# Rows of the first expert tile selected on TensorE, with shorter routing arithmetic

## The chip, the cores and the metric

The kernel runs on one core of one Trainium2 chip. The metric is the time of one execution on the device in microseconds (us). TensorE does the matrix products, VectorE and ScalarE the elementwise work, GpSimd starts the indexed transfers, SyncE starts the large loads. Times inside the program are taken from one profiled execution and count from the start of its span.

## The reference, cut to what matters

A block of 512 tokens of width 1024: a modulated norm, a mixing layer, a residual sum, a second modulated norm that gives `hf`, and a mixture of 16 experts of which each token takes two. Only the last part is touched.

```
def grouped_moe(h, router_w, router_bias, w_gate, w_up, w_down):
    logits = t @ router_w                              # 512 x 16
    probs = softmax(logits); sel = (probs + bias) in 4 groups of 4
    group_score = sum of the 2 best of each group; g_idx = argmax
    e_idx = the 2 best experts of that group
    wts = probs of these two, divided by their sum
    a = silu(t @ w_gate[e]) * (t @ w_up[e]) * combine[:, e]
    y = sum over e of a @ w_down[e]
```

## The kernel before

All arithmetic is float32. A wide product is made of three passes (`three`, L1363 to L1365): each operand is split into a rounded part "hi" (type float32r, made on ScalarE) and a remainder "lo" (made on VectorE, L771), and hi*hi, hi*lo and lo*hi are summed in PSUM. Weights arrive in `raw` (six slots of 128x2048) and their two parts stand in `wsplit` (six slots as well).

The stage in question lies between 424 and 481 us. TensorE transposes the normed rows `hf` (L1548) and makes the router logits (L1537). VectorE then does the routing: softmax, `rank` of the four experts of each group (L1103 to L1113; six instructions, with two comparisons and two multiplications by a table `order` so that ties fall the right way), the sum of the two best, `rank` of the four groups, and the mask of chosen experts `r_m` (L1130). From the mask TensorE counts each token's place in its expert's list (L1562, L1564, with full float32 operands), and VectorE writes the place to `pos1` (L1151).

Tokens are handled in tiles of 128 rows of one expert. Tile 0 is expert 0's first 128 rows, tile 1 expert 1's; the rest of the table (which expert and which rows each of the up to 24 tiles has, in `expert_of`, `base`, `weights_of`) is worked out on VectorE (L1183 to L1229) and released with `tiles_ready`. For every tile the steps are:

- VectorE makes a selection matrix `sel` (`select`, L1160: four instructions of 128x128, one for each 128 tokens);
- TensorE multiplies it with `info` (`index`, L1573), which gives the token number, weight and destination of each row; VectorE copies them out (`indices`, L1168 to L1170);
- GpSimd gathers the rows of `hf` from a copy in HBM into `hg` (`gather`, L461);
- TensorE turns the rows (`turn`, L1583), ScalarE writes the hi part of `hgT` (L683), VectorE the lo part (`rows_lo`, L1175);
- TensorE makes gate and up (`gate_up`: four chunks of 12 products with 512 columns), the hidden part is formed (L1238), turned (L1617) and multiplied by the down weights.

The order on each engine is written by hand. On TensorE it is `index(0,0)`, `index(1,1)`, `turn(0)`, `gate_up(0)`, then `index(2)`, `turn(1)`, `turn_hidden(0)`, then `gate_up(1)` and the loop. On VectorE, the selection of tile 0 comes first, then the table in pieces, with the lo parts of the two up chunks of tile 0 (`lo_n(M0 + 2)`, `lo_n(M0 + 3)`) among them; after `tiles_ready` come `select(2)`, three lo parts, `hidden(0)`, `indices(2)`, a fourth lo part and `rows_lo(1)`, on which `gate_up(1)` waits (`hg_lo`).

Semaphores count finished steps: `hi_ready`, `lo_ready` (split chunks), `chunk_used` (products done with a chunk), `sel_ready`, `idx_mm`, `idx_ready`, `gathered`, `hg_t`, `hg_hi`, `hg_lo`. `step` and `done` on VectorE chain dependent small instructions.

## Time and profile before

| | us |
|---|---|
| median of three runs | 804.03 |
| lowest and highest | 803.33, 804.06 |
| the profiled execution, whole | 805.07 |
| its span | 803.3 |
| TensorE matmul busy in the span | 735.6 (92%) |
| VectorE busy | 589.2 (73%) |
| ScalarE busy | 389.6 (49%) |
| GpSimd busy | 192.8 (24%) |

The profiled execution took 1.04 us more than the median. The span is what the trace covers. Busy shares are means over stages with different limits, so the stage around a change has to be read from the trace: the chain of waits says which engine released which, the timeline gives the instructions of one engine in order, and a table of stretches gives busy time and the TensorE clock that was granted (1.00 is 2.4 GHz, 0.50 is 1.2 GHz).

### The profile page before, as it was taken

To read this page: it belongs to the slowest core of one execution; us is meant where nothing else is said; L and a number is where in the kernel's file an instruction comes from. 1 tells how busy PE (TensorE), PEld (TensorE's weight loads), DVE (VectorE), ACT (ScalarE), POOL (GpSimd) and SP (SyncE) were. 2 spreads that over 40 slices of the span, in tenths; PEclk is the share of its full clock that TensorE was granted. 3 is DMA by queue.
4 is the path that set the end of the run, shared out by engine and by line. 5 is a ranking of instruction groups with operands and counts; after the bars stand their busy time and mean duration, and the time that the engine had idled before them with its cause. 6 is when DMAs were issued, how large, how long until landed. Compare 5 with 4: busy or idle time off the path is not lost. (4 is left out here: it accounts for less than half of the span.)

```text
span 803.3 us, 10622 instructions
## 1 busy us (share of the span) xinstructions
PE 735.6 (92%) x3359; PEld 606.1 (75%) x3360; DVE 589.2 (73%) x789; ACT 389.6 (49%) x352; POOL 192.8 (24%) x79
## 2 busy tenths in 40 slices
PE   2589999999999999999998389999999999999990
PEld 2468888866888888886788278888888888888880
DVE  3762344765485766668464788999999999999955
ACT  6442523343323241415234266777777777777723
POOL 1000001401000000000062101445555555444532
PEclk9689999999999999999997589999999999999996
DMA  8796330431365564726464428599999999999685
GB/s 323 271 371 218 104 131 15 143 104 53 107 217 179 171 216 138 280 87 259 160 227 142 163 79 310 203 354 407 370 358 375 358 360 380 371 373 381 249 170 165
DMA packets 105651, 187.66 MB, mean 234 GB/s; under 512 B 6991, under 2 KB 50063, under 8 KB 105628
## 3 DMA queue, kind: packets, MB, share of 16 engines
q1 hardware_dynamic: 98076, 173.58, 59.6%
q0 software_dynamic: 5936, 12.14, 5.5%
q10 hardware_dynamic: 1616, 1.65, 0.6%
q8 instruction: 13, 0.21, 0.1%
q14 instruction: 10, 0.08, 0.0%
HBM read 180.47 MB, written 16.25 MB: 245 GB/s over the span
## 5 line engine op out<-in xcount | busy, mean ns | idle before, releaser
L771 DVE TENSOR_TENSOR wsplit<-raw,wsplit 128x2048 fp32r<-128x2048 f32 x132 | 298.9, 2284 | 81.0 <-ACT wsplit L521 53.5
L700 ACT ACTIVATE wsplit<-raw 128x2048 fp32r<-128x2048 f32 x96 | 184.0, 1920 | 73.5 <-PE ps L1365 73.5
L469 POOL DMA_INDIRECT expert_rows<-work,dest_now x15 | 108.2, 7210 | 113.5 <-DVE work L1256 113.5
L1363 PE MATMUL ps<-wsplit,hgT 128*128 128x512 f32 x280 | 112.7, 403 | 5.0 <-DVE hgT L1175 5.0
L1365 PE MATMUL ps<-wsplit,hgT 128*128 128x512 f32 x280 | 110.9, 396 | 0.0
L1364 PE MATMUL ps<-wsplit,hgT 128*128 128x512 f32 x280 | 110.6, 395 | 0.0
L1363 PE MATMUL ps<-hT,wsplit 128*128 128x512 f32 x256 | 101.0, 395 | 1.0 <-DVE mx L929 1.0
L1365 PE MATMUL ps<-hT,wsplit 128*128 128x512 f32 x256 | 99.6, 389 | 0.0
L1364 PE MATMUL ps<-hT,wsplit 128*128 128x512 f32 x256 | 99.6, 389 | 0.0
L828 DVE SCALAR_TENSOR_TENSOR raw<-raw,c_silu 128x256 f32 (+1 forms) x128 | 62.0, 484 | 12.9 <-DMA raw<-in_w_ada 8.9
L1363 PEld LDWEIGHTS ps<-wsplit,hgT 128*128 128x128 f32 x280 | 53.7, 192 | 16.5 <-DVE hgT L1175 5.7
L1365 PEld LDWEIGHTS ps<-wsplit,hgT 128*128 128x128 f32 x280 | 53.5, 191 | 11.8
L1364 PEld LDWEIGHTS ps<-wsplit,hgT 128*128 128x128 f32 x280 | 53.8, 192 | 10.9
L1363 PE MATMUL ps<-wsplit,hT 128*128 128x512 f32 x128 | 52.8, 412 | 8.3 <-DVE hT L877 6.8
L477 POOL TENSOR_TENSOR wsplit<-raw,wsplit 128x2048 fp32r<-128x2048 f32 x2 | 9.2, 4610 | 200.6 <-ACT wsplit L521 200.5
L1363 PEld LDWEIGHTS ps<-hT,wsplit 128*128 128x128 f32 x256 | 48.1, 188 | 11.7 <-issue 1.9
L640 ACT ACTIVATE wsplit<-raw 128x2048 fp32r<-128x2048 f32 x16 | 30.7, 1918 | 53.4 <-PE ps L1365 34.8
L1364 PEld LDWEIGHTS ps<-hT,wsplit 128*128 128x128 f32 x256 | 48.1, 188 | 10.4 <-issue 0.7
L521 ACT ACTIVATE wsplit<-raw 128x2048 fp32r<-128x2048 f32 x20 | 38.2, 1915 | 36.5 <-PE ps L1365 14.0
L1365 PEld LDWEIGHTS ps<-hT,wsplit 128*128 128x128 f32 x256 | 48.0, 188 | 10.1
L1364 PE MATMUL ps<-wsplit,hT 128*128 128x512 f32 x128 | 51.8, 405 | 0.0
L1365 PE MATMUL ps<-wsplit,hT 128*128 128x512 f32 x128 | 51.8, 404 | 0.0
(257 smaller groups left out, 1190.5 us busy)
## 6 DMA issues: line engine op xcount, KB each, us to landing
raw<-in_w_exp_gate SPq DMA_DIRECT2D x32, 1024.0 KB
raw<-in_w_exp_up SPq DMA_DIRECT2D x32, 1024.0 KB
raw<-in_w_exp_down SPq DMA_DIRECT2D x32, 1024.0 KB
raw<-in_w_ada SPq DMA_DIRECT2D x24, 1024.0 KB
raw<-in_w_in SPq DMA_DIRECT2D x20, 1024.0 KB
expert_rows<-tmp SPq DMA_DIRECT2D x4, 1024.0 KB, 12.3
raw<-in_w_branch_a SPq DMA_DIRECT2D x4, 1024.0 KB
raw<-in_w_branch_b SPq DMA_DIRECT2D x4, 1024.0 KB
```

Source lines behind the costliest of these rows:

```text
L469: g.indirect_dma_start(out=y_dram, out_offset=bass.IndirectOffsetOnAxis(ap=dest_now[:, 0:1], axis=0), in_=y, in_offset=None, bounds_check= ...
L477: g.tensor_tensor(wsplit[:, c + 2, 1, :], raw[:, c + 2, :], wsplit[:, c + 2, 0, :].bitcast(F32), ALU.subtract).then_inc(lo_ready, 1)
L521: A_(wsplit[:, n, 0, :], raw[:, slot, :], ACT.Copy).then_inc(hi_ready, 1)
L640: A_(wsplit[:, (j + 1) % 2, 0, :], raw[:, (j + 1) % 4, :], ACT.Copy).then_inc(hi_ready, 1)
L700: A_(wsplit[:, c, 0, :], raw[:, c, :], ACT.Copy).then_inc(hi_ready, 1)
L771: V.tensor_tensor(wsplit[:, n, 1, :], raw[:, slot, :], wsplit[:, n, 0, :].bitcast(F32), ALU.subtract).then_inc(lo_ready, 1)
L828: ins = V.scalar_tensor_tensor(out=acc, in0=raw[:, slot, k * CC:(k + 1) * CC], scalar=c_silu[:, k:k + 1], in1=acc, op0=ALU.mult, op1=ALU.add)
L1363: nc.tensor.matmul(out, w_hi, m_hi_, start=first, stop=False)
L1364: nc.tensor.matmul(out, w_hi, m_lo_, start=False, stop=False)
L1365: return nc.tensor.matmul(out, w_lo, m_hi_, start=False, stop=last)
```

## The change

- Tile 0's rows are no longer gathered. After the second norm ScalarE writes the hi part of each 128 rows of `hf` to `wsplit` slots 1 and 0 and VectorE the lo part (`hf_part`; 4 copies and 4 subtractions of 128x1024). TensorE multiplies them with the selection matrix `sel_first` (`first_rows`: 2 halves x 2 parts x 4 blocks x 4 token groups = 64 products with 128 columns), which gives the turned rows at once. Hi and lo parts are copied out by ScalarE and VectorE, 512 columns at a time.
- `index(0,0)` and `index(1,1)` move behind the first chunk of `gate_up(0)`, which is written out so that its chunks wait for halves of the rows.
- The ranking is a subtraction, one comparison with a table `beats` (0 or the least normal number) and a sum. A threshold and a multiplication become one instruction in two places.
- The place products take float32r operands (`before_r`, `ones_r`, `r_mask`).
- On VectorE the selection of tile 0 comes before the weights' arithmetic, and the whole table comes behind the rows of tile 0; `lo_n(M0 + 3)` moves ahead of the table's last part.
- SyncE waits also for the lo parts of `hf` before it loads over `hf`. Semaphore counts of `gathered` are one less.

```
@@ sync
             sp.wait_ge(hf_t, 2 * NT)
+            sp.wait_ge(hs_lo, NT)
             for c in range(2):
                 load(c + 4, w_up[0, :, 4 * c:4 * c + 4, :], 4)
@@ gpsimd
-            for j in range(4):
+            for j in range(1, 4):
                 gather(j)
@@ scalar
+            def rows_split(t):
+                act.wait_ge(hf_ready, t + 1)
+                act.wait_ge(chunk_used, O0 + 2 if t < 2 else M0 - 1)
+                A_(hf_part(t, 0), hf[:, t, :], ACT.Copy).then_inc(hs_hi, 1)
...
-            rows_hi(0)
+            for half in range(2):
+                act.wait_ge(row0_mm, 2 * half + 1)
+                A_(hgT[:, 0, 4 * half:4 * half + 4, :].rearrange("p k m -> p (k m)"), ps[:, 2 + half, :],
+                   ACT.Copy).then_inc(hg_hi if half else row0_hi, 1)
+            act.wait_ge(hg_t, 1)
@@ vector
+            for t in range(NT):
+                dve.wait_ge(hs_hi, t + 1)
+                V.tensor_tensor(hf_part(t, 1), hf[:, t, :], hf_part(t, 0).bitcast(F32),
+                                ALU.subtract).then_inc(hs_lo, 1)
...
-                step(V.tensor_tensor(r_ge[:, 0:n], other, mine, ALU.is_ge))
-                step(V.tensor_tensor(r_gt[:, 0:n], other, mine, ALU.is_gt))
+                step(V.tensor_tensor(r_ge[:, 0:n], other, mine, ALU.subtract))
...
+                step(V.tensor_tensor(r_ge[:, 0:n], r_ge[:, 0:n], beats[:, :, :].unsqueeze(1).broadcast_to(pair),
+                                     ALU.is_ge))
...
+            def first_rows_lo(half):
+                dve.wait_ge(hg_t if half else row0_mm, 1 if half else 2)
+                V.tensor_copy(hgT[:, 1, 4 * half:4 * half + 4, :].rearrange("p k m -> p (k m)"),
+                              ps[:, 5 + half, :]).then_inc(hg_lo if half else row0_lo, 1)
@@ tensor
-            nc.tensor.matmul(ps[:, 2, 0:(NT + 1) * E], before[:, :], r_m_all, start=True, stop=False)
+            nc.tensor.matmul(ps[:, 2, 0:(NT + 1) * E], before_r[:, :], r_mask[:, :], start=True, stop=False)
...
-            index(0, 0)
-            index(1, 1)
-            turn(0)
-            gate_up(0, M0, 2)
+            def first_rows(half):
+                for part in range(2):
+                    for k in range(4 * half, 4 * half + 4):
+                        for t in range(NT):
+                            mm = nc.tensor.matmul(ps[:, (2, 5)[part] + half, (k % 4) * P:(k % 4 + 1) * P],
+                                                  hf_part(t, part)[:, k * P:(k + 1) * P], sel_first[:, t, :],
+                                                  start=(t == 0), stop=(t == NT - 1))
+                    mm.then_inc(hg_t if half and part else row0_mm, 1)
+
+            pe.wait_ge(sel_ready, 1)
+            pe.wait_ge(hs_lo, NT)
+            first_rows(0)
+            first_rows(1)
+            for c in range(4):
+                half = c % 2
+                pe.wait_ge(hg_hi if half else row0_hi, 1)
+                pe.wait_ge(hg_lo if half else row0_lo, 1)
+                pe.wait_ge(lo_ready, M0 + c + 1)
+                for k in range(4):
+                    kk = 4 * half + k
+                    mm = three(ps[:, c // 2, :], hgT[:, 0, kk, :], hgT[:, 1, kk, :],
+                               wblock(2 + c, 0, k, 512), wblock(2 + c, 1, k, 512), kk == 0, kk == ND - 1)
+                mm.then_inc(chunk_used, 1)
+                if c == 0:
+                    index(0, 0)
+                    index(1, 1)
```

How this moves instructions is seen at two places. The first is TensorE from the place products to the start of tile 0's gate product. In these rows `ps<-info,sel` are the index products and `ps<-ident,work` the turning of gathered rows. Before:

```order
L1562 MATMUL ps<-work,before 128x80
L1564 MATMUL ps<-work,ones 128x64
L1564 MATMUL ps<-work,ones 128x48
L1564 MATMUL ps<-work,ones 128x32
L1564 MATMUL ps<-work,ones 128x16
L1573 MATMUL ps<-info,sel 128x4 x8
L1583 MATMUL ps<-ident,work 128x128 x8
L1363 MATMUL ps<-wsplit,hgT 128x512
```

On TensorE after, from the same place (`ps<-sel_first,wsplit` are the 64 selecting products):

```order
L1606 MATMUL ps<-r_mask,before_r 128x80
L1608 MATMUL ps<-r_mask,ones_r 128x64
L1608 MATMUL ps<-r_mask,ones_r 128x48
L1608 MATMUL ps<-r_mask,ones_r 128x32
L1608 MATMUL ps<-r_mask,ones_r 128x16
L1676 MATMUL ps<-sel_first,wsplit 128x128 x64
L1407 MATMUL ps<-wsplit,hgT 128x512
```

The eight index products have left this place; they stand twelve gate products later, on TensorE after the first chunk:

```order
L1409 MATMUL ps<-wsplit,hgT 128x512
L1622 MATMUL ps<-info,sel_first 128x4 x4
L1622 MATMUL ps<-info,sel 128x4 x4
L1407 MATMUL ps<-wsplit,hgT 128x512
```

The second place is VectorE behind the selection of tile 0, where L771 (before) and L798 (after) are the lo parts of weight chunks. Before, the selection of tile 1 and the first part of the table stand ahead of tile 0's rows:

```order
L1160 TENSOR_SCALAR sel<-iota,base,pos 128x128 x4
L1189 TENSOR_TENSOR work<-work 128x16
L1190 TENSOR_SCALAR work<-work 128x16
L1192 TENSOR_TENSOR work<-work 128x16
L1194 TENSOR_SCALAR work<-work 128x1
L1196 MEMSET work 128x1
L1198 SCALAR_TENSOR_TENSOR work<-ones,work 128x16
L771 TENSOR_TENSOR wsplit<-raw,wsplit 128x2048
L1203 TENSOR_TENSOR work<-iota,work 128x384
L1206 TENSOR_REDUCE work<-work 128x24
L1208 TENSOR_TENSOR work<-work 128x384
```

On VectorE after, the rows of tile 0 (L1223, twice) come first, and the table starts behind them:

```order
L1198 TENSOR_SCALAR sel<-iota,base,pos 128x128 x4
L1223 CAST hgT<-ps 128x512
L798 TENSOR_TENSOR wsplit<-raw,wsplit 128x2048
L1223 CAST hgT<-ps 128x512
L1230 TENSOR_SCALAR work<-work 128x16
L1231 TENSOR_SCALAR work<-work 128x16
L1232 TENSOR_SCALAR work<-work 128x16
L1234 TENSOR_TENSOR work<-work 128x16
L1235 TENSOR_SCALAR work<-work 128x16
L1237 TENSOR_TENSOR work<-work 128x16
L1239 TENSOR_SCALAR work<-work 128x1
L1241 MEMSET work 128x1
```

What moved: the whole table now stands behind the second row copy, which waits for the last of the 64 products; before it stood mostly beside the gather.

## Rows read from the trace of the kernel before

**Rows 1.** Chain of waits, 452 to 481 us: start, us, engine and line.

```profile
452.58 5.03 DMA work<-hf_rows,tok_idx
457.65 1.98 PE ps L1583 x8
...
461.99 0.80 PE ps L1363
...
467.90 0.30 PE ps L1364
...
475.72 0.24 PE ps L1365
...
480.32 0.50 PE ps L1363
```

**Rows 2.** Stretches: length, busy PE, PEld, DVE, ACT, POOL, PEclk, DMA, GB/s.

```profile
480.00:485.00 5.00, 4.68 (x14) 3.69 (x15) 5.00 (x4) 2.52 (x4) 0.00 (x0) 0.66 0.27 46
...
600.00:760.00 160.00, 160.00 (x778) 133.92 (x777) 159.45 (x158) 117.70 (x79) 85.87 (x18) 1.00 0.97 362
```

**Rows 3.** Timeline of VectorE, routing: start, us, operation, idle before it.

```profile
441.26 0.42 DVE L1103 TENSOR_TENSOR work<-work 128x256 f32<-128x256 f32 x1
...
443.77 0.19 DVE L1121 TENSOR_SCALAR work<-work 128x64 f32<-128x64 f32 x1
...
444.51 0.22 DVE L1103 TENSOR_TENSOR work<-work 128x64 f32<-128x64 f32 x1
...
446.02 0.22 DVE L1130 TENSOR_TENSOR work<-work 128x64 f32<-128x64 f32 x1
...
448.65 0.22 DVE L1151 SCALAR_TENSOR_TENSOR pos<-ps,work 128x64 f32<-128x64 f32 x1 [0.30 <-PE ps L1564]
...
448.99 1.11 DVE L1160 TENSOR_SCALAR sel<-iota,base,pos 128x128 fp32r<-128x128 f32 x4
```

**Rows 4.** Timeline of TensorE: place products and logits.

```profile
430.63 3.60 PE L1537 MATMUL ps<-router,work 128*128 128x16 f32 x16 [0.25 <-ACT work L245]
...
446.80 1.81 PE L1564 MATMUL ps<-work,ones 128*128 128x64 f32 x8
```

**Rows 5.** Timelines of VectorE, ScalarE and SyncE, 431 to 440 us.

```profile
439.48 0.23 DVE L1083 TENSOR_REDUCE work<-ps 128x4 f32<-128x64 f32 x1 [7.92 <-PE ps L1537]
...
435.19 0.60 ACT L245 ACTIVATE work<-ps 128x512 f32<-128x512 f32 x1 [4.13 <-PE ps L1548]
...
436.26 0.94 SPq L278 DMA_DIRECT2D raw<-in_w_exp_up  x2
```

**Rows 6.** All instructions of L1452: duration, first and last start, form.

```profile
L1452 PE MATMUL ps<-tmp,raw x64: 270/275/275, 130.7 to 137.7; 128*128 128x128 f32 x64
```

**Rows 7.** Stretches of 1 us at the kernel's start (columns as in rows 2).

```profile
14.00:15.00 1.00, 0.90 (x5) 0.93 (x6) 0.95 (x2) 1.00 (x2) 0.00 (x0) 1.00 1.06 412
...
18.00:19.00 1.00, 1.00 (x12) 1.00 (x11) 0.96 (x3) 0.00 (x0) 0.00 (x0) 1.00 1.06 412
```

**Rows 8.** Timeline of VectorE, table and tile 1.

```profile
452.49 0.17 DVE L1189 TENSOR_TENSOR work<-work 128x16 f32<-128x16 f32 x1
...
453.57 2.29 DVE L771 TENSOR_TENSOR wsplit<-raw,wsplit 128x2048 fp32r<-128x2048 f32 x1
455.78 0.55 DVE L1203 TENSOR_TENSOR work<-iota,work 128x384 f32<-128x384 f32 x1
...
461.85 0.54 DVE L1212 TENSOR_REDUCE work<-work 128x24 f32<-128x384 f32 x1
...
463.71 2.29 DVE L771 TENSOR_TENSOR wsplit<-raw,wsplit 128x2048 fp32r<-128x2048 f32 x1
465.92 1.11 DVE L1160 TENSOR_SCALAR sel<-iota,base,pos 128x128 fp32r<-128x128 f32 x4
...
476.04 0.69 DVE L1238 TENSOR_TENSOR work<-ps,work 128x512 f32<-128x512 f32 x1 [0.77 <-PE ps L1365]
...
476.85 2.28 DVE L771 TENSOR_TENSOR wsplit<-raw,wsplit 128x2048 fp32r<-128x2048 f32 x1
```

More of the change, by code:

```diff
@@ L45 @@
 SKIP = 2048
+LEAST = 1.1754943508222875e-38
 FIN_X = (4, 5, 6, 8)
@@ L93, in tokens_moe_kernel @@
         mx = sb("mx", [P, NT * D])
+        with nc.sbuf_tensor("sel_first", [P, NT, P], F32R) as sel_first:
+            pass
         tmp = sb("tmp", [P, 2 * D])
         iota1 = sb("iota1", [P, P])
+        before_r = sb("before_r", [P, P], F32R)
+        ones_r = sb("ones_r", [P, P], F32R)
+        r_mask = sb("r_mask", [P, (NT + 1) * E], F32R)
         router = sb("router", [P, ND, E])
@@ L108, in tokens_moe_kernel @@
         bias_row = sb("bias_row", [P, E])
-        order = sb("order", [P, 2, EG, EG])
+        beats = sb("beats", [P, EG, EG])
         pos1 = sb("pos1", [P, NT, E])
@@ L180, in tokens_moe_kernel @@
                   "pos_mm", "tiles_ready"))
+        hs_hi, hs_lo, row0_mm, row0_hi, row0_lo, info_ready = map(
+            sem, ("hs_hi", "hs_lo", "row0_mm", "row0_hi", "row0_lo", "info_ready"))
         sel_ready, idx_mm, idx_ready, gathered, hg_t, hg_hi, hg_lo = map(
@@ L215, in tokens_moe_kernel @@
         r_gs, r_gr = small(NT * EG), small(NT * EG)
-        r_ge, r_gt = (small(NT * E * EG).rearrange("p (g a b) -> p g a b", a=EG, b=EG) for _ in range(2))
+        r_ge = small(NT * E * EG).rearrange("p (g a b) -> p g a b", a=EG, b=EG)
         r_cnt, r_x, r_x2, r_x3, r_cum = (small(E) for _ in range(5))
@@ L237, in mix_lo, with hf_part @@
                                        op1=ALU.subtract).then_inc(yb_lo, 1)
+        def hf_part(t, part):
+            return wsplit[:, 1 - t // 2, part, (t % 2) * D:(t % 2 + 1) * D]
         def turned(act, activation, t):
@@ L424, in _ @@
             g.memset(eps_col[:, :], EPS)
-            g.memset(order[:, :, :, :], 1.0)
+            g.memset(beats[:, :, :], 1.0)
             g.iota(iota_i[:, :], pattern=[[1, P]], base=1, channel_multiplier=0)
@@ L459, in gather @@
                 wait_reg(pool, idx_ready, j + 1)
-                wait_reg(pool, hg_t, j, 0)
+                if not isinstance(j, int) or j > 1:
+                    wait_reg(pool, hg_t, j)
                 g.indirect_dma_start(out=hg, out_offset=None, in_=hf_dram,
@@ L672, in _ @@
                    scale=1.0 / D).then_inc(rooted, 1)
-            for t in range(2, NT):
-                turned(act, A_, t)
+                if t:
+                    rows_split(t - 1)
+            turned(act, A_, 2)
+            rows_split(NT - 1)
+            turned(act, A_, 3)
             act.wait_ge(sub_ready, 1)
@@ L1077, in _ @@
             step(V.memset(r_m_all[:, NT * E:], 0.0))
+            step(V.tensor_copy(before_r[:, :], before[:, :]))
+            step(V.tensor_copy(ones_r[:, :], ones[:, :]))
+            done()
+            step(V.tensor_copy(r_mask[:, NT * E:], r_m_all[:, NT * E:]))
             lg = ps[:, 4, 0:NT * E].rearrange("p (t e) -> p t e", t=NT)
@@ L1120, in _ @@
             rank(sel_g, NT * EG, top_g)
+            step(V.scalar_tensor_tensor(out=r_m, in0=r_top, scalar=2.0, in1=r_sel, op0=ALU.is_lt, op1=ALU.mult))
             step(V.tensor_scalar(r_top, r_top, 2.0, None, ALU.is_lt))
-            done()
-            step(V.tensor_tensor(r_m, r_sel, r_top, ALU.mult))
             done()
@@ L1147, in _ @@
             done()
-            step(V.tensor_tensor(info[:, :, :, 2], r_p3, info[:, :, :, 1].bitcast(F32), ALU.subtract))
-            dve.wait_ge(pos_mm, 1)
-            step(V.scalar_tensor_tensor(out=pos1[:, :, :], in0=ps[:, 2, 0:NT * E].rearrange("p (t e) -> p t e", t=NT),
-                                        scalar=1.0, in1=r_m3, op0=ALU.add, op1=ALU.mult))
-            step(V.tensor_copy(r_cnt, ps[:, 2, NT * E:NT * E + E]))
-            done()
+            V.tensor_tensor(info[:, :, :, 2], r_p3, info[:, :, :, 1].bitcast(F32),
+                            ALU.subtract).then_inc(info_ready, 1)
             def select(j, e):
-                dve.wait_ge(idx_mm, j)
+                if not isinstance(j, int) or j > 1:
+                    dve.wait_ge(idx_mm, j)
                 for t in range(NT):
@@ L1186, in _ @@
             done()
-            indices(0)
-            select(1, 1)
             step(V.tensor_tensor(r_x, r_x, r_x2, ALU.add))
@@ L1209, in _ @@
             done()
+            indices(0)
             indices(1)
-            rows_lo(0)
+            lo_n(M0 + 3, 5)
             step(V.tensor_reduce(r_first, r_le, AX_X, ALU.max))
@@ L1568, in index @@
             def index(j, e):
+                first = isinstance(j, int) and j == 0
+                col = 4 if isinstance(j, int) and j == 1 else 0
                 pe.wait_ge(sel_ready, j + 1)
-                pe.wait_ge(idx_ready, j)
+                if not isinstance(j, int) or j > 1:
+                    pe.wait_ge(idx_ready, j)
+                else:
+                    pe.wait_ge(info_ready, 1)
                 for t in range(NT):
-                    mm = nc.tensor.matmul(ps[:, 7, 0:4], sel[:, t, :],
+                    mm = nc.tensor.matmul(ps[:, 7, col:col + 4], (sel_first if first else sel)[:, t, :],
                                           info[:, t, ds(e, 1), :].rearrange("p a n -> p (a n)"),
```

61 lines of the change are left out of this document (35 added, 26 removed).

## The prediction

> **What bounds the kernel now.** I read the stretches first, then the chain of waits, then the timelines of the stage in which the work changes. From 600 to 760 us TensorE is busy 160.00 of 160.00 us at the full clock [rows 2]: the expert loop runs as fast as TensorE, and VectorE, busy 159.45, has almost no slack either. The change leaves the loop alone, so what counts is when the loop's work can start. I take the first product of `gate_up(1)` as the marker: 480.32 us [rows 1]. A shift there is carried to the end one to one, as far as the clock that follows is the same.
>
> The chain up to that marker has three parts. The routing on VectorE runs from 441.26 to the selection at 448.99 [rows 3]. Then come the gather, 5.03 us, the turning, 1.98 us, the two copies, and `gate_up(0)` from 461.99 to 475.96 [rows 1]. Last, VectorE's hidden part at 476.04, a lo part and the rows of tile 1 lead from TensorE's end to 480.32 [rows 8, 1].
>
> **The change, part by part.**
>
> Splitting `hf`. Four copies on ScalarE (about 1.1 us each by the 0.60 of 512 columns) and four subtractions on VectorE (about 1.2 us each, twice the 0.6 of 512 columns in rows 8), 4.9 us, plus three small copies. VectorE had 7.92 us without work there and ScalarE 4.13 us before its last two turned blocks [rows 5]; the first three copies fall into earlier gaps. The subtractions end near 436.3, when SyncE issues its next loads anyway [rows 5]: the new wait costs it 0 to 0.5 us, and nothing waits for those loads. I take 0. Without the cover the subtractions would cost 4.9 us.
>
> Routing. One step of 256 elements takes its 0.42 us and 0.04 to the next, one of 64 elements 0.26. The first ranking, 441.26 to 443.77 = 2.51 us, becomes three steps, 1.38: 1.13 saved. The second, with its threshold, 444.51 to 446.02 = 1.51, becomes 0.78: 0.73 saved. The multiplication joined with the first threshold gives 0.1. Together 2.0 us [rows 3], with little doubt since these are the same kinds of instructions.
>
> Place products. Eight passes take 1.81 us, 0.226 each [rows 4]; the five products are two passes each before and one after, so five passes fewer are 1.1 us. No row shows a float32r product of 16 to 80 columns: bounds 0 to 1.1. I take 1.1, because a pass of 16 columns costs 3.60 / 16 = 0.225 [rows 4], so the columns do not set the price. The first selecting product then starts near 448.99 + 1.11 + 0.06 - 2.0 - 1.1 = 447.1 us.
>
> Selecting. It replaces index, copies, gather, turning and a copy between 450.1 and 461.99, 11.9 us, by 64 products of 128 columns. Their pitch is not in the trace in this type; the nearest rows are the passes of 128 columns in full float32 at the high clock, (137.7 - 130.7) / 63 = 0.111 us [rows 6], and the narrow passes at the low clock, 0.215 without the last one's latency [rows 4]. The far bounds are the passes of 512 columns, 5.11 us for the 12 left out, 0.426 slow [rows 1], and 0.227 fast; I stay at the near rows, since narrower passes cost no less than these. So the 64 take 64 x 0.111 = 7.1 us at the high clock and 64 x 0.215 = 13.8 us at the low one. Everything hangs on which it is.
>
> The clock. TensorE was at the low clock before this point: the logits run at 0.225 a pass [rows 4] and `gate_up(0)` at 0.426 until 467.90, 5.9 us after its start, then at 0.23 to 0.24 [rows 1]. The first transposes of the kernel, also 128 columns, doubled their rate: 5 starts in the first 0.9 us, 12 in the fifth [rows 7] (the clock column has 1.00 in both and does not settle it, the starts do), about 3.3 us after the first. Against that, the logits' 16-column passes went on for 3.60 us at the same pitch, with as many weight loads, and stayed slow [rows 4]. A selecting product is like the transposes in width, but not in type: full float32 needs two passes for a product of this width [rows 6], the selection one. I take it that this stream does not raise the clock, which puts it with the logits, and I am in real doubt about it. As the time from the start of a stream that does raise it to the rise I take 4.6 us, the middle of 3.3 and 5.9.
>
> The Trainium skill (TensorE: Matmul & The Clock Gate, Part 4) says that transposes do not bring the high clock; rows 7 disagree, with 5 starts in a microsecond becoming 12. By that sentence the high clock at the kernel's start would have no cause here; the sum does not use it.
>
> The selection at the low clock thus ends at 447.1 + 13.8 = 460.9. The first gate chunk, 12 products, takes 4.6 us slow (10.8 of them) and 0.3 fast: 465.8. The eight index passes, now here, cost 0.9, and 0.35 until VectorE sees them: 467.0.
>
> VectorE after the selection. It may copy rows only at the selection's end: 0.3 latency, 0.65 copy (like the 0.69 of 512 columns from PSUM in rows 8), 0.27 for three comparisons, 453.57 - 452.49 = 1.08 and three instructions of 0.55, 1.75, for the table's first pieces [rows 8]: 4.05 us, here 464.95, so it waits for the index at 467.0. Then a fixed queue: two `indices` 0.4, a lo part 2.2 (453.57 to 455.78), the table's rest 463.71 - 461.85 = 1.86, the selection of tile 2 1.03, three lo parts 6.6, hidden part and indices 476.85 - 476.04 = 0.81, the fourth lo part and the rows of tile 1, 480.32 - 476.85 = 3.47 [rows 8]. Sum 16.4 us. The queue never waits for TensorE: that ends `gate_up(0)` at 466.7 + 36 x 0.227 = 474.9, while VectorE reaches the hidden part at 479.1. Marker: 467.0 + 16.4 = 483.4, against 480.32: **+3.1 us**. In the kernel before, the table and a lo part lay beside the gather and the slow products; now they lie behind them.
>
> After the marker. TensorE is idle for most of 7 us before it, so the clock is low at its start. Before, the clock was low for part of 480 to 485: the mean 0.66 means 3.4 of 5 us at half rate [rows 2], 1.7 us lost. After, 4.6 us at half rate lose 2.3: +0.6, bounds 0 to 1.2. What is moved past GpSimd is nothing new: the gather of tile 1 is issued at about 467.4, lands by 473.5, before its turning.
>
> Sum: +3.1 + 0.6 = +3.7, taken as **+3.5** because the rise may come sooner in a stream that is already running. The profiled execution, 805.07, goes to 808.6, and the median, 804.03, to **807.5**. Its own range is 806.0 to 809.3: a rise after 3.3 us instead of 4.6 shortens the first gate chunk by 0.6 and the loss behind the marker by 0.65; one after 5.9 us makes the chunk 0.2 and the index 0.9 longer and the loss 0.65 larger.
>
> **The rivals.**
>
> Rival 1, faster: the selecting stream raises the clock. For it speak the transposes of rows 7; against it the logits of rows 4. It runs 4.6 us slow (21.4 products) and 42.6 x 0.111 = 4.7 fast: end at 456.4, marker 456.4 + 4.05 + 16.4 = 476.8, -3.5; with +0.6 behind the marker -2.9: 801.1, between 800.0 and 802.3. It decides from a selection of 12.2 us: with that the end is at 459.3, the marker at 479.7, and the gain of 0.6 is what the clock takes back behind it. The Trainium skill (TensorE: Matmul & The Clock Gate, Part 1) tells of back-to-back products of 128 columns that reach the high clock in mid-stream, which is this rival's mechanism. No run here shows it for this type.
>
> Rival 2, slower by another road: the clock rises, but a float32r product of 128 columns costs as much as one of 512, 0.227 fast. Then the selection takes 4.6 + (64 - 10.8) x 0.227 = 15.8 us, ends at 462.9, and the marker is 483.3: +3.0 and 0.6, 807.6. Only the full price for 512 columns in rows 1 allows it; rows 6 speak against it.
>
> Rival 3, no change: VectorE's queue is shorter than my sum, or the clock rises late in the selection, and gains and losses cancel: 803 to 805. The change not doing what it says would be this case as well: if the loop, not its start, set the time, a shift of the marker would be swallowed. Rows 2, with TensorE full, speak against it.
>
> **How the numbers follow.** The forecast has 0.54, rival 1 0.32, rival 2 0.05, rival 3 0.09. The predicted time is the likeliest one's, 807.5 us. Leaving out about 1 in 10 on each side, the range must reach into rival 1: 800.4 to 809.3. About 0.2% (1.6 us) is what a measurement of this kernel can tell from no change. Faster by more: rival 1, 0.32 with a little of rival 3, less its weak end: 0.32. Slower by more: 0.58. Within: 0.10.
>
> **What would show it.** In the profile of the changed kernel: the first selecting product near 447.1; its pitch 0.215 throughout (forecast) or halving on the way (rival 1), or 0.43 (rival 2); the granted clock 0.50 to 461 or 1.00 from some 452; VectorE without a gap from the index copies to the rows of tile 1; the marker at 483.4 or 476.8; TensorE idle between the end of `gate_up(0)` and the marker for some 7 us; from there the same 160.00 of 160.00. The forecast is wrong if the clock is high before 457, or if `gate_up(1)` starts while VectorE still has table work, which the order excludes.

## The result, and the profile after

| | before | changed |
|---|---|---|
| median of six runs each, us | 804.46 | 808.72 |
| lowest and highest | 803.33, 805.67 | 807.04, 809.46 |
| ratio, 95% interval | | 1.005 (1.0037 to 1.0064) |
| profiled execution, whole | 805.07 | 808.42 |
| its span | 803.3 | 806.5 |
| start of `gate_up(1)`, the marker | 480.32 | 483.93 |
| first index product of the tile loop | 492.96 | 497.02 |

The change makes the kernel 0.5% slower, 4.3 us. The forecast was 3.5 us slower, 807.5 us, by a selection that stays at TensorE's low clock. The busy times of the changed kernel hardly differ from those of before: TensorE has 10.6 us more, and its clock row (40 slices of the span, 20.2 us each) shows 6, 5, 8 and 8 between 423 and 504 us, where the stage in question lies.

```profile
span 806.5 us, 10729 instructions
PE 746.2 (93%) x3410; PEld 617.1 (77%) x3411; DVE 592.7 (73%) x789; ACT 394.1 (49%) x357; POOL 192.9 (24%) x78
...
PEclk9689999999999999999996588999999999999996
```

The chain of waits of the changed kernel, from the mask to the marker (start, us, engine and line), answers [rows 1]:

```profile
443.72 0.23 DVE r_mask L1158
...
445.34 0.23 DVE pos L1169
...
445.68 1.12 DVE sel_first L1175 x4
...
446.85 13.91 PE ps L1676 x64
460.76 0.53 PE ps L1407
...
465.34 0.79 PE ps L1622 x8
...
483.93 0.79 PE ps L1407
```

In place of the gather's 5.03 us and the 1.98 of turning there is one piece of 13.91 us, the 64 selecting products. The stretches give the clock below it (length, busy PE, PEld, DVE, ACT, POOL, PEclk, DMA, GB/s):

```profile
448.00:450.00 2.00, 2.00 (x11) 2.00 (x10) 1.39 (x6) 0.00 (x0) 0.00 (x0) 0.50 0.00 0
...
458.00:460.00 2.00, 2.00 (x11) 2.00 (x11) 0.00 (x0) 0.00 (x0) 0.00 (x0) 0.50 0.86 276
...
480.00:485.00 5.00, 2.19 (x7) 1.60 (x8) 5.00 (x7) 1.56 (x2) 2.25 (x1) 0.50 0.02 1
485.00:490.00 5.00, 5.00 (x17) 3.92 (x16) 4.90 (x7) 0.92 (x1) 0.00 (x0) 0.67 0.53 165
...
600.00:760.00 160.00, 160.00 (x779) 133.92 (x778) 159.51 (x159) 118.02 (x79) 88.06 (x18) 1.00 1.00 371
```

TensorE was busy for all of the selection and the granted clock was 0.50 for all of it, with 11 or 12 products in every 2 us. It rose only in the gate products behind, at about 464.4, where the chain's pieces of L1407 to L1409 go from 0.43 to 0.24 us. The last row answers [rows 2]: the loop is as full as before.

VectorE's timeline shows where the table went (start, us, operation, idle before it), as [rows 8] did:

```profile
453.98 0.69 DVE L1223 CAST hgT<-ps 128x512 fp32r<-128x512 f32 x1 [4.55 <-PE ps L1676]
454.58 2.28 DVE L798 TENSOR_TENSOR wsplit<-raw,wsplit 128x2048 fp32r<-128x2048 f32 x1
460.80 0.69 DVE L1223 CAST hgT<-ps 128x512 fp32r<-128x512 f32 x1 [3.94 <-PE ps L1676]
...
466.23 0.16 DVE L1210 TENSOR_REDUCE row_w<-ps 128x1 f32<-128x2 f32 x1 [1.69 <-PE ps L1622]
...
466.90 2.28 DVE L798 TENSOR_TENSOR wsplit<-raw,wsplit 128x2048 fp32r<-128x2048 f32 x1
...
472.02 1.12 DVE L1198 TENSOR_SCALAR sel<-iota,base,pos 128x128 fp32r<-128x128 f32 x4 [1.08 <-issue]
473.05 6.69 DVE L798 TENSOR_TENSOR wsplit<-raw,wsplit 128x2048 fp32r<-128x2048 f32 x3
```

VectorE waits three times for TensorE, 4.55 + 3.94 + 1.69 = 10.2 us. The first pieces of its table stand between the second and the third wait, and only behind the third come the rest of the table and five of its six lo parts. TensorE in its turn waits for VectorE when `gate_up(0)` is done:

```profile
480.40 1.12 PE L1666 MATMUL ps<-ident,work 128*128 128x128 f32 x4 [4.10 <-DVE work L1282]
483.93 0.79 PE L1407 MATMUL ps<-wsplit,hgT 128*128 128x512 f32 x1 [2.41 <-DVE hgT L1216]
```

The two engines take turns in waiting. That, besides the slow products, is what the experiments below turn on.

### The profile page after: what moved, and what is told of

It is laid out like the page before. It is cut to its first block, busy times and chain, and to the rows that moved or that the text cites. A ratio compares the mean times of both kernels' runs of the same rounds, so it can differ in the third digit from the quotient of the medians.

```text
span 806.5 us, 10729 instructions
## 1 busy us (share of the span) xinstructions
PE 746.2 (93%) x3410; PEld 617.1 (77%) x3411; DVE 592.7 (73%) x789; ACT 394.1 (49%) x357; POOL 192.9 (24%) x78
## 4 chain that ended last, share of the span: by engine, by line
PE 58%; DMA 24%; DVE 10%; issue 3%; DVEq 1%; ACT 1%; SPq 0%; POOLq 0%; POOL 0%; ACTq 0%
DMA expert_rows<-work,dest_now 20%; PE ps L1407 17%; PE ps L1408 17%; PE ps L1409 17%; DMA mx<-expert_rows 3%; DVE wsplit L798 2%; DVE work L1300 2%; PE ps L1676 2%; DVE raw L883 1%; PE ps L1508 1%; PE ps L1581 1%; DMA raw<-in_w_ada 1%; DMA raw<-in_w_out 1%; PE ps L1421 1%; DVEq L1326 1%
## 5 line engine op out<-in xcount | busy, mean ns | idle before, releaser
L798 DVE TENSOR_TENSOR wsplit<-raw,wsplit 128x2048 fp32r<-128x2048 f32 x132 | 299.1, 2286 | 79.8 <-ACT wsplit L535 53.8
L1407 PE MATMUL ps<-wsplit,hgT 128*128 128x512 f32 x280 | 112.5, 402 | 2.4 <-DVE hgT L1216 2.4
L1409 PE MATMUL ps<-wsplit,hgT 128*128 128x512 f32 x280 | 110.6, 395 | 0.0
L1407 PE MATMUL ps<-hT,wsplit 128*128 128x512 f32 x256 | 101.0, 395 | 1.0 <-DVE mx L956 1.0
L1409 PE MATMUL ps<-hT,wsplit 128*128 128x512 f32 x256 | 99.6, 389 | 0.0
L1407 PEld LDWEIGHTS ps<-wsplit,hgT 128*128 128x128 f32 x280 | 53.7, 192 | 13.5 <-DVE hgT L1216 2.8
L1409 PEld LDWEIGHTS ps<-wsplit,hgT 128*128 128x128 f32 x280 | 53.4, 191 | 11.7
L1407 PE MATMUL ps<-wsplit,hT 128*128 128x512 f32 x128 | 52.5, 410 | 7.9 <-DVE hT L904 6.8
L1407 PEld LDWEIGHTS ps<-hT,wsplit 128*128 128x128 f32 x256 | 48.1, 188 | 11.9 <-issue 1.9
L1409 PEld LDWEIGHTS ps<-hT,wsplit 128*128 128x128 f32 x256 | 48.0, 188 | 10.0
L475 POOL DMA_INDIRECT work<-hf_rows,tok_idx x17 | 36.4, 2142 | 68.1 <-DVE row_dest L1211 55.8
L1408 PE MATMUL ps<-wsplit,hT 128*128 128x512 f32 x128 | 51.7, 404 | 0.0
```

What stands on the lines that cost most here:

```text
L475: g.indirect_dma_start(out=hg, out_offset=None, in_=hf_dram, in_offset=bass.IndirectOffsetOnAxis(ap=tok_idx[:, 0:1], axis=0), bounds_check ...
L798: V.tensor_tensor(wsplit[:, n, 1, :], raw[:, slot, :], wsplit[:, n, 0, :].bitcast(F32), ALU.subtract).then_inc(lo_ready, 1)
L1407: nc.tensor.matmul(out, w_hi, m_hi_, start=first, stop=False)
L1408: nc.tensor.matmul(out, w_hi, m_lo_, start=False, stop=False)
L1409: return nc.tensor.matmul(out, w_lo, m_hi_, start=False, stop=last)
```

## The experiments

The stage starts at a slightly different time in each profiled execution: VectorE's first ranking instruction lies between 439.86 and 441.93 us in the ten profiles, whatever the edit. So the profiles are compared by two distances: from the first ranking instruction to the marker, and from the marker to the loop's first index product. From there every profile has the same 18.1 to 18.2 us for the next tile. A shift of their sum against before should be the shift of the time, and it nearly is. Each ratio is to executions of the kernel before that were measured beside that kernel: their medians are 804.46 us for the changed kernel, 803.82 for e1 to e4, 803.72 for e5 and e6, 803.52 for e7 and e8. The ratio is not the quotient of the two medians; for e7 and e8 that quotient is 0.0013 and 0.0014 higher, elsewhere it is within 0.0005.

| kernel | ranking to marker | marker to loop | sum against before | median, us | ratio to before, 95% interval |
|---|---|---|---|---|---|
| before | 39.06 | 12.64 | | | |
| changed | 42.98 | 13.09 | +4.4 | 808.72 | 1.005 (1.0037 to 1.0064) |
| e1 routing only, gathered | 35.67 | 12.64 | -3.4 | 801.05 | 0.9963 (0.9951 to 0.9975) |
| e2 clock raised beforehand | 34.15 | 13.89 | -3.7 | 800.13 | 0.9956 (0.9939 to 0.9973) |
| e3 table early | 38.16 | 11.05 | -2.5 | 801.73 | 0.997 (0.9954 to 0.9987) |
| e4 two passes | 43.35 | 12.62 | +4.3 | 808.65 (one) | |
| e5 clock and table | 33.15 | 12.62 | -5.9 | 797.96 | 0.9927 (0.9911 to 0.9944) |
| e6 gathered, clock raised | 33.21 | 12.51 | -6.0 | 797.45 | 0.9924 (0.9907 to 0.9941) |
| e7 clock held to the marker | 33.90 | 11.05 | -6.8 | 796.5 | 0.99 (0.9879 to 0.9921) |
| e8 order mended | 32.21 | 13.08 | -6.4 | 797.7 | 0.9914 (0.9892 to 0.9937) |

The theory: the selection is slow because its stream does not bring the high clock, and it costs time because the table stands behind it on VectorE. The rivals: that the routing edits gain nothing, that such a product is slow at either clock, and that VectorE's order does not matter.

**e1_routing_only.** The kernel before with the short rankings and the place products in float32r, the gather kept.

```
-                step(V.tensor_tensor(r_ge[:, 0:n], other, mine, ALU.is_ge))
-                step(V.tensor_tensor(r_gt[:, 0:n], other, mine, ALU.is_gt))
+                step(V.tensor_tensor(r_ge[:, 0:n], other, mine, ALU.subtract))
...
-            nc.tensor.matmul(ps[:, 2, 0:(NT + 1) * E], before[:, :], r_m_all, start=True, stop=False)
+            nc.tensor.matmul(ps[:, 2, 0:(NT + 1) * E], before_r[:, :], r_mask[:, :], start=True, stop=False)
```

> The kernel before, with only the shorter rankings and the one-pass place products; tile 0 is still gathered. My theory (the routing parts gain what they save, the selection loses the rest): the selection matrix of tile 0 is ready 3.1 us earlier, everything behind it moves along, gate_up(1) starts near 477 instead of 480.3, and the time is about 801.3, 3.1 under the kernel before. Rival (the stage behind is bound by something else, a weight transfer or VectorE's queue, so the earlier mask buys nothing): within 0.5 us of the kernel before.

Measured: 801.05 us, 0.9963 (0.9951 to 0.9975), as expected. The gathered rows reach TensorE 3.7 us earlier in the profile, and the marker follows (timeline of TensorE):

```profile
453.98 1.97 PE L1589 MATMUL ps<-ident,work 128*128 128x128 f32 x8 [3.27 <-DMA work<-hf_rows,tok_idx]
...
476.37 0.50 PE L1369 MATMUL ps<-wsplit,hgT 128*128 128x512 f32 x1 [2.64 <-DVE hgT L1181]
```

From the ranking to the marker the stage is 3.4 us shorter. Of that, 2.4 us lie before the first index product, which comes 6.52 us after the first ranking instruction instead of 8.90. Another 0.7 lies in the gather, which took 4.3 us from issue to landing and 5.0 in the kernel before; the edit does not touch it, and why it was shorter is open. By the times, the routing half of the change gains about 3 us (0.9951 to 0.9975, so 2.0 to 3.9) and the selecting half by itself loses about 7: 42.98 + 13.09 against 35.67 + 12.64 is 7.8 in the profiles, 808.72 against 801.05 is 7.7 in the medians of two groups of runs, and the ratios give (1.005 - 0.9963) x 804 = 7.0.

**e2_warm.** The changed kernel with products that nothing reads, 11 between the logits and the mask and 5 behind the place products.

```
+            def dummies(n):
+                for _ in range(n):
+                    nc.tensor.matmul(ps[:, 7, :], wsplit[:, 2, 0, 0:P], wsplit[:, 2, 0, 0:512], start=True, stop=True)
+
+            pe.wait_ge(lo_ready, M0 + 1)
+            dummies(11)
             pe.wait_ge(mask_ready, 1)
...
             mm.then_inc(pos_mm, 1)
+            dummies(5)
```

> The changed kernel, with 11 idle products of 512 columns on TensorE between the logits and the mask and 5 between the place products and the selection; their result is not used. They bring TensorE to the high clock before the 64 selecting products. My theory (the low clock makes the selection long, its pitch follows the clock): the pitch falls from 0.217 to about 0.111, the selection takes 7.1 instead of 13.9 us, gate_up(1) starts near 474.5 instead of 483.9, and the time is about 799.5. If the one-pass stream cannot hold the high clock either, it falls on the way or just behind, the first gate chunk is slow, and the gain is 3 to 5 us. Rival (the pitch is set by the weight loads from SBUF and not by the clock): pitch stays near 0.21, the time stays at 808.7 or is worse.

Measured: 800.13 us, 0.9956 (0.9939 to 0.9973). TensorE's timeline and two stretches of the selection:

```profile
437.87 4.99 PE L1607 MATMUL ps<-wsplit 128*128 128x512 f32 x11
...
445.25 7.36 PE L1683 MATMUL ps<-sel_first,wsplit 128*128 128x128 f32 x64 [0.36 <-DVE sel_first L1175]
```

```profile
446.00:448.00 2.00, 2.00 (x21) 2.00 (x19) 1.75 (x8) 0.60 (x1) 0.00 (x0) 1.00 0.00 0
...
470.00:480.00 10.00, 7.10 (x18) 5.45 (x19) 9.98 (x13) 2.20 (x3) 2.25 (x1) 0.50 0.27 82
```

The same 64 products take 7.36 us, 0.115 each, at 1.00, against 13.91 at 0.50. So the product is not slow by its kind (rival 2 of the prediction); it is slow by the clock. The stream keeps a high clock that it finds, though it does not bring one. The marker comes 8.8 us sooner, but then the clock is low for the whole of 470 to 480, and the marker-to-loop distance is 0.8 longer.

**e3_table_early.** The changed kernel, its clock untouched, with VectorE's whole table before the rows of tile 0.

```
             select(1, 1)
-            first_rows_lo(0)
-            lo_n(M0 + 2, 4)
-            first_rows_lo(1)
             step(V.tensor_scalar(r_x, r_cnt, float(P), None, ALU.is_gt))
...
-            indices(0)
-            indices(1)
-            lo_n(M0 + 3, 5)
...
             dve.wait_ge(tiles_ready, 1)
+            first_rows_lo(0)
+            lo_n(M0 + 2, 4)
+            lo_n(M0 + 3, 5)
+            first_rows_lo(1)
+            indices(0)
+            indices(1)
```

> The changed kernel, with VectorE's whole tile table and lo_n(M0 + 3) put ahead of the second row copy, where VectorE idles 4.55 and 3.94 us. My theory (behind the selection VectorE's queue is the bound, so what is taken out of it counts in full): the 1.86 us of the table's rest, the 2.2 us of the lo part and what waits ahead of the index leave the queue; gate_up(1) starts near 479 instead of 483.9, the time is 803.5 to 805. Rival (TensorE's slow selection and first chunk alone set the time, VectorE merely follows): no change, 808 to 809.

Measured: 801.73 us, 0.997 (0.9954 to 0.9987). The selection is as slow as in the changed kernel, `13.92` for the 64, and still the time is 7 us shorter than that of the changed kernel, and shorter than the 803.5 to 805 that were expected:

```profile
447.46 13.92 PE L1676 MATMUL ps<-sel_first,wsplit 128*128 128x128 f32 x64 [1.62 <-DVE sel_first L1175]
...
474.88 0.50 PE L1622 MATMUL ps<-info,sel 128*128 x4
...
476.19 0.66 PE L1666 MATMUL ps<-ident,work 128*128 128x128 f32 x4
479.72 0.50 PE L1407 MATMUL ps<-wsplit,hgT 128*128 128x512 f32 x1 [2.88 <-DVE hgT L1216]
```

TensorE goes straight from `gate_up(0)` to the index, the turning and the hidden part; only 2.88 us of waiting are left of 6.5. The ranking-to-marker distance falls by 4.8, and the marker, 479.72, is near the 479 of the expectation. Behind the marker the clock stays at 1.00, which was not expected, and gives 2.0 more. On the table's scale e3 thus gains 6.9 us where e2 gains 8.0; of this the order on VectorE explains the 4.8, while the 2.0 come by a clock that the edit was not meant to change.

**e4_two_pass.** The selecting products on operands that are read as full float32.

```
-                                                  hf_part(t, part)[:, k * P:(k + 1) * P], sel_first[:, t, :],
+                                                  hf_part(t, part)[:, k * P:(k + 1) * P].bitcast(F32),
+                                                  sel_first[:, t, :].bitcast(F32),
```

> The changed kernel, with the 64 selecting products as full float32, that is two passes of 128 columns each, 128 passes in all; the values are the same. My theory of the clock (the one-pass stream does not raise it, a two-pass stream of the same width does, as at the kernel's start): the clock rises 3.3 to 5.9 us after the first selecting product, the 128 passes take 15 to 18 us in place of 27.4, the first gate chunk runs fast, and gate_up(1) starts near 484, the time is within 2 us of the changed kernel. Rival (128 columns never raise it, whatever the type): 27.4 us of selection at 0.214 a pass, gate_up(1) near 497, the time about 822.

Measured: 808.65 us in the one execution that there is, beside executions of before between 801.97 and 805.79. Twice the passes take 16.12 us against 13.91:

```profile
446.00 16.12 PE L1676 MATMUL ps<-sel_first,wsplit 128*128 128x128 f32 x128 [1.62 <-DVE sel_first L1175]
```

```profile
446.00:448.00 2.00, 2.00 (x9) 2.00 (x10) 1.86 (x11) 0.00 (x0) 0.00 (x0) 0.50 0.01 2
448.00:450.00 2.00, 2.00 (x14) 2.00 (x13) 0.55 (x3) 0.00 (x0) 0.00 (x0) 0.68 0.00 0
450.00:452.00 2.00, 2.00 (x20) 2.00 (x19) 0.00 (x0) 0.57 (x1) 0.00 (x0) 1.00 0.00 0
```

Here the clock does rise in mid-stream: a mean of 0.68 in a stretch that starts at 0.50 and ends at 1.00 puts the rise at 449.3, 3.3 us after the first product. In the one-pass streams of the changed kernel and of e3 it did not rise in 13.9 us. This is the question on which the forecast and rival 1 parted. The same matrices, with a weight load for each pass in both, and 9 starts in the first 2 us against 11 in a stretch of the changed kernel, raise the clock as full float32 and not as float32r. The edit changes the type and the number of passes together, so e4 (one profile) does not say which of the two it is. The transposes of [rows 7] speak against the number of passes: each is one record, 32 for 32 transposes, and their starts rose from 5 to 12 in a microsecond all the same (the clock column has 1.00 in both rows, so this rests on the starts).

```profile
14.10 5.27 PE L1386 MATMUL ps<-ident,mx 128*128 128x128 f32 x32 [9.92 <-ACT mx L547]
```

The Trainium skill (TensorE: Matmul & The Clock Gate, Part 1) tells of a stream of bf16 products of 128 columns that reaches the high clock in mid-stream. The stream of e4 does the same, after 3.3 us; the changed kernel's, in float32r, does not in its 13.91 us at 0.50.

**e5_warm_table.** The edits of e2 and e3 together.

> The changed kernel with both: the idle products that bring the high clock before the selection, and the table and lo_n(M0 + 3) ahead of the second row copy. My theory (clock and queue are two separate costs that add): gate_up(1) starts near 468.5, 5.5 us before the warm kernel's 474.0, and the time is about 795. Rival (both cures work on the same wait, so together they give little more than the better one): 798.5 to 800.

Measured: 797.96 us, 0.9927 (0.9911 to 0.9944), the marker at 473.96, not at 468.5. The time lies between the 795 of the theory and the 798.5 to 800 of its rival, nearer to the rival. The expectation took one from the other as if each had a wait of its own to remove. From the ranking to the loop e2 saves 8.0 us over the changed kernel and e3 6.9, the two together 10.3. The chain of waits shows what came instead:

```profile
453.56 0.97 issue
...
457.54 0.79 PE ps L1629 x8
458.32 1.21 issue
...
462.32 0.43 PE ps L1409
```

Two new waits of TensorE, 0.97 and 1.21 us, stand in it, and behind them the clock falls: from 460.6 to 464.0 the gate products take 0.43 us each instead of 0.23, which costs about 1.6 us more. VectorE finishes the table at 453.7 and copies the first half of the rows then, though it had been ready since about 450; the second half is ready at 453.6 and copied at 458.75, behind two lo parts:

```profile
453.74 0.69 DVE L1223 CAST hgT<-ps 128x512 fp32r<-128x512 f32 x1
...
458.75 0.68 DVE L1223 CAST hgT<-ps 128x512 fp32r<-128x512 f32 x1
```

`gate_up(0)` ends at 469.6, and VectorE then waits 0.89 us for it before the hidden part. The order of e3 was right for a selection of 14 us and is wrong for one of 7.

**e6_gather_warm.** e1 with the same idle products, and more of them around the turning, so that the gathered version has a high clock in its gate products too.

```
             index(1, 1)
+            dummies(14, 1)
             turn(0)
+            dummies(8, 1)
             gate_up(0, M0, 2)
```

> The kernel before with the shorter routing, tile 0 gathered, and idle products of 512 columns on TensorE in the gaps up to gate_up(0) (11 and 5 as in the warm kernel, 14 before the turning, 8 before the first gate product). My theory: the gather chain itself does not depend on the clock except for index and turning (2 us), gate_up(0) runs at 0.227 throughout, so its end moves from 472.0 to about 468 and gate_up(1) from 476.4 to about 472.5: about 797.5, which says that with the clock held the gather is as good as the selection or better. Rival (selection beats the gather once the clock is equal for both): this kernel stays at 800 or above, over the warm selection's 800.1.

Measured: 797.45 us, 0.9924 (0.9907 to 0.9941). With a high clock for `gate_up(0)`, gathering is not worse than selecting (e2 and e5). The first five lines are TensorE's, the last two the issue of the gather and VectorE's copy of tile 0's rows:

```profile
448.52 0.61 PE L1586 MATMUL ps<-info,sel 128*128 128x4 f32 x4 [1.47 <-DVE sel L1166]
448.98 5.05 PE L1569 MATMUL ps<-wsplit 128*128 128x512 f32 x14
453.87 1.03 PE L1596 MATMUL ps<-ident,work 128*128 128x128 f32 x8
454.66 2.09 PE L1569 MATMUL ps<-wsplit 128*128 128x512 f32 x8
457.29 0.50 PE L1369 MATMUL ps<-wsplit,hgT 128*128 128x512 f32 x1 [0.54 <-DVE hgT L1181]
...
448.46 1.10 POOL L466 DMA_INDIRECT work<-hf_rows,tok_idx  x1 [9.29 <-issue]
...
456.01 1.23 DVE L1181 TENSOR_TENSOR hgT<-ps,hgT 128x1024 fp32r<-128x1024 f32 x1 [2.28 <-ACT hgT L688]
```

`gate_up(0)` starts at 457.29, 17.4 us after the first ranking instruction; in e2, with the selection, it starts at 452.45, 12.6 after it. Yet e2's marker comes 0.9 us later than e6's on the same scale (34.15 against 33.21). The 4.8 us that TensorE is ahead in e2 it spends waiting for VectorE: 3.94 and 2.42 us behind `gate_up(0)`, against 2.87 in e6. The gather leaves VectorE free for the table; the selection needs it for two copies at times of its own.

e6 is not the best that the gather can do. Its clock was at 0.50 from 449.0 to 452.5, inside the 14 idle products, so these ended only at 454.0. The gather, issued at 448.46, landed 4.3 to 4.4 us later, at about 452.8, and the turning stood behind the idle products until 453.87, 1.0 us too late. VectorE waited for the rows of tile 0 (2.28 us, above) and had no further wait up to the marker, so by the trace this 1.0 us passes on to the marker. No run with fewer idle products tests it.

**e7_hold.** e6 with nine more idle products behind the turning of tile 0's hidden part.

```
             turn_hidden(0)
+            pe.wait_ge(lo_ready, M0 + 5)
+            for _ in range(9):
+                nc.tensor.matmul(ps[:, 1, :], wsplit[:, 0, 0, 0:P], wsplit[:, 0, 0, 0:512], start=True, stop=True)
```

> The kernel of e6 (gathered rows, short routing, clock held by idle products), with nine more idle products of 512 columns behind the turning of tile 0's hidden part, that is in front of gate_up(1), while TensorE waits for the rows of tile 1. In e6 TensorE was idle for 2.87 us there and gate_up(1) began at the low clock, seven products at 0.43 instead of 0.23 and part of an eighth. If only the clock is at stake, the nine (2.0 us) lie inside the wait, the marker stays at 473.1, its products are at 0.227 from the first on, and the time falls by 1.5 us, 797.45 to about 796.0. The rival: what is saved behind the marker is lost in the loop's first tiles, where VectorE is then the one that is late; then 797.2 to 797.5 with idle TensorE time between 480 and 500.

Measured: 796.5 us, 0.99 (0.9879 to 0.9921), from 795.38 to 799.27. The highest is the profiled one, so its absolute times say little, but the place is plain:

```profile
472.71 2.32 PE L1648 MATMUL ps<-wsplit 128*128 128x512 f32 x9
475.83 0.50 PE L1369 MATMUL ps<-wsplit,hgT 128*128 128x512 f32 x1 [0.80 <-DVE hgT L1181]
```

```profile
476.00:478.00 2.00, 2.00 (x9) 1.62 (x10) 2.00 (x2) 1.61 (x2) 0.00 (x0) 1.00 0.04 2
```

From the marker to the loop it is 11.05 us against 12.51 in e6: the 1.5 us of the low clock are gone, as expected, and none comes back in the first tiles, so the rival expected of this run falls. In this profile 0.7 was lost earlier, where the clock was at 0.50 from 448.2 to 455.0: the index products ran at it, and the idle products behind them held the turning 1.4 us beyond the gather's landing. The intervals of e6 and e7 overlap, so by the time alone the gain is not shown. e7 has the lowest median and ratio of all, 1.0% under before, but the intervals of e6 and e8 overlap with its own.

**e8_order_mended.** e5 with VectorE's two copies and lo parts between the scan and the table's wide steps.

```
             ie = [P, TILES_MAX, E]
+            first_rows_lo(0)
+            lo_n(M0 + 2, 4)
+            first_rows_lo(1)
+            lo_n(M0 + 3, 5)
...
             dve.wait_ge(tiles_ready, 1)
-            first_rows_lo(0)
-            lo_n(M0 + 2, 4)
-            lo_n(M0 + 3, 5)
-            first_rows_lo(1)
             indices(0)
             indices(1)
```

> The kernel of e5 (changed kernel, clock held by idle products, table early), but with VectorE's two copies of the first rows and the two lo parts put between the scan and the table's wide steps, so that each copy stands in the queue where the fast selection has its half ready (450.4 and 453.6). If the order was what cost e5 its gain, the first gate chunk starts near 453.9, gate_up(0) ends near 465.5 with no stall, the marker is at 473 (bounded by VectorE's five lo parts and the hidden part behind the table, which ends near 459) and the time about 797.0, against 797.96 of e5. If the order did not matter, since VectorE has the same work before the marker either way, the marker stays at 474.0 and the time at 798.0.

Measured: 797.7 us, 0.9914 (0.9892 to 0.9937). The copies now stand where the halves are ready, and TensorE runs on without a stall up to the end of `gate_up(0)`:

```profile
450.43 0.69 DVE L1223 CAST hgT<-ps 128x512 fp32r<-128x512 f32 x1
...
453.93 0.69 DVE L1223 CAST hgT<-ps 128x512 fp32r<-128x512 f32 x1 [0.62 <-PE ps L1683]
```

```profile
466.11 1.10 PE L1639 MATMUL ps<-ident,work 128*128 128x128 f32 x8
469.83 0.66 PE L1673 MATMUL ps<-ident,work 128*128 128x128 f32 x4 [2.62 <-DVE work L1282]
473.36 0.79 PE L1407 MATMUL ps<-wsplit,hgT 128*128 128x512 f32 x1 [2.87 <-DVE hgT L1216]
```

`gate_up(0)` is done at 465.8 instead of 469.6, and the marker comes 0.9 us sooner on the scale of the table, about as expected. Half of that goes again behind the marker (13.08 against 12.62): TensorE, done earlier, waits longer, 2.62 and 2.87 us, and `gate_up(1)` begins with 4.4 us at the low clock against 3.4 in e5. The time, 797.7, lies between the 797.0 expected and the 798.0 of its rival; in the medians the difference from e5, 0.3 us, can't be told from none. From the ranking to the marker e5, e6, e7 and e8 take 32.2 to 33.9 us, whichever way the rows come. VectorE is busy for 29.4 or 29.5 us of these in all four, with six lo parts in each.

## Why the prediction was right, point by point

The time was 808.72 for 807.5, the marker 483.93 for 483.4, and the mechanism was the forecast one: the selection at the low clock, and behind it VectorE's table. By its steps:

- **Splitting `hf`.** Taken as hidden. SyncE issued its loads at 435.76, not later than the 436.26 of [rows 5]. The cover held.
- **Routing and place products.** 2.0 and 1.1 us. From the first ranking instruction to the place products it was 5.04 us [rows 3, 4] and is now 444.00 - 440.95 = 3.05: 1.99 saved. From there to the read of the places it was 2.35 and is 1.34: 1.01 saved. The upper bound of the second term was right: the products took 2.31 us in ten passes before and take 1.24 in five. e1 shows the first saving without the selection, 3.04 us for 5.04. Of the second it shows 0.4: the products end 1.1 us sooner there too, but VectorE reads the places only at 445.72, 0.7 us behind their end, since the weights' arithmetic still stands ahead of the read.
- **The selection.** 13.8 us from 447.1; measured 13.91 from 446.85. The slow pitch, 0.217, lies at the logits' 0.215 [rows 4], and e2's fast one, 0.115, lies at the 0.111 of [rows 6]: both far rows, the 512-column ones, were no guide.
- **The clock.** The forecast put the one-pass stream with the logits and against the transposes of [rows 7] with 0.54 to 0.32. The changed kernel and e3 bear out that this stream does not raise the clock, e4 that the same matrices in full float32 do. The odds were little better than even, and the reason given was only half right: it set the two passes of full float32 against the one of the selection, but the transposes of [rows 7] have one pass each. Whether it is the type, and how the chip weighs it, is open.
- **Rival 2.** Its sum is wrong: 4.6 + 53.2 x 0.227 is 16.7 us, not 15.8, which puts the end of the selection at 463.8 and the time at 808.5. Its time could thus not have been told from the forecast's; the pitch of 0.217, and e2's 0.115, rule it out.
- **The first gate chunk and the index.** 4.9 us and 0.9 + 0.35; measured 4.58, and 0.79 + 0.10. VectorE had its index at 466.23 instead of 467.0, of which 0.3 is the earlier start of the whole stage in this profile.
- **VectorE's queue.** 16.4 us; measured 483.93 - 466.23 = 17.7. This is the term that was mis-sized, and the sign asked for, VectorE without a gap up to the rows of tile 1, did not come. Two gaps have no work of VectorE in them: 0.24 us inside the index copies and 1.08 us before the selection of tile 2. The same instructions are in the kernel before, where no such gap shows: a lo part stood there, between the table's end and this selection [rows 8]. In the changed kernel that lo part has moved ahead of the table's end and the gap lies bare; in e8, with five small instructions between, 0.64 of it is left; in e5, with two copies and two lo parts between, none. The profile calls it issue. That it is the reading of tile 2's expert number into a register, which the order of the program suggests, is argued and not shown.
- **The gather of tile 1.** Taken as landed before its turning; TensorE waited 0.43 us for it, at 475.20. It then waited 4.10 us for VectorE, so this cost nothing.
- **Behind the marker.** +0.6 for the lower clock; the marker-to-loop distance went from 12.64 to 13.09, +0.45.
- **One to one to the end.** The loop's first index product is 4.06 us later, VectorE's last instruction only 799.87 - 796.70 = 3.17. The tail gave 0.9 back in this execution. The medians, +4.3, show none of it, and in the ten profiles the distance from the loop's start to that instruction lies anywhere from 302.7 to 304.4 us, so it is scatter more than a gain.

The errors of the sum, -0.8 at the index, +1.3 in the queue and -0.9 at the tail, cancel for the most part; that the marker lies within 0.5 us of the forecast is in part luck. Its mechanism, a slow selection with the table behind it, is no luck: e2 and e3 take it away each in its own way.

What the prediction did not see is how the two halves hang together. It priced rival 1 with all of the table still behind the selection, and e2 confirms that only in part: the marker fell by 8.8 us, where the prediction has 483.4 - 476.8 = 6.6 with a clock that rises on the way, while a clock that is high from the start takes 6.5 off the selection and 1.8 off the first chunk (2.80 us in e2's chain for 4.58). But no term asked what the selection could bring at best, with clock and order right. e5, e6 and e8 answer: nothing that can be measured over the gather of e6, which itself loses about 1.0 us to its idle products. VectorE's queue stands before the marker either way.

## What to carry to other kernels

Before a wait for a transfer is replaced by work on an engine, look at what the other engines do in the wait: here VectorE made its table beside the gather, and the new work, which took turns with VectorE, pushed the table behind it. An engine's hand-written order belongs to the durations that it was written for; when one of them halves, the order has to be looked at again, and two gains that remove the same wait don't add. And a stage between two waits is worth running a few idle products in, if the engine's clock is low at its end: with the gather kept, that brought as much again as the shorter routing (ratios 0.9924 and 0.9963). They have to be fewer than the wait holds at the low clock, or they delay the work behind them.

## What the runs showed of the hardware

- A stream of one-pass float32r products of 128 columns, each with its own weights, ran for 13.91 us at the low clock without raising it, and for 7.36 us at the high clock without losing it. The same stream in full float32, two passes a product, raised it after 3.3 us, so that twice the passes cost only 2.2 us more. Type and number of passes were changed together.
- A wait of the same length left different clocks behind. With 2.88 us idle before `gate_up(1)` e3 went on at 1.00; with 2.87 us e6 began it at 0.50. The kernel before, with 2.64 us, began it high and fell 1.3 us later; e5, with 2.64 us as well, fell within 0.4 us of the start. A saving that counts on a clock kept over such a wait is not sure; e7's products in the wait made it 1.00 from the first product on.
- Idle products of 512 columns did not slow the other engines: e6 puts 38 of them in the stage and no step of VectorE there is longer than in e1. In TensorE's own queue they are not free: 14 of them took 5.05 us, part of it at the low clock, and held the turning 1.0 us beyond the gather's landing in e6, 1.4 us in e7.
